# The other order of the experts and early lower results, with a fifth slot in the ring of split weight pairs, in the expert stage of a two-layer decoder trunk

## The reference

```
xn = rms_norm(x)                                   # 512 tokens, 1024 columns, float32
group  = the best of 4 groups (softmax p_group)
e1, e2 = the best two of the group's 4 experts, softmaxed and scaled by p_group
for e in 16 experts:
    hid = silu(xn @ w_gate[e]) * (xn @ w_up[e])    # 1024 -> 256
    y  += gates[:, e] * (hid @ w_down[e])          # 256 -> 1024
x = x + y
```

## Time and profile before

| | us |
|---|---|
| median of three runs (lowest, highest) | 1561.42 (1557.63, 1564.19) |
| the profiled execution's own time | 1558.49 |
| its span | 1556.6 |
| PE busy | 1458.1 |
| DVE busy | 935.9 |
| ACT busy | 866.0 |
| POOL busy | 457.7 |

### The profile page before, as it was taken

How to read it: one execution, slowest core, us unless ns; L and a number is a source line. 1 busy time by engine, 2 the same in 40 slices (tenths; PEclk the granted TensorE clock), 3 DMA queues, 4 the chain that set the end, 5 groups by cost and what they waited for, 6 DMA issues and landing times.

```text
span 1556.6 us, 22096 instructions
## 1 busy us (share of the span) xinstructions
PE 1458.1 (94%) x7676; PEld 1128.2 (72%) x7676; DVE 935.9 (60%) x1824; ACT 866.0 (56%) x1668; POOL 457.7 (29%) x638
## 2 busy tenths in 40 slices
PE   7999999999999996999699999999999999889993
PEld 6887777677777785777578877766777777667772
DVE  3555654644554446999754565645454535579996
ACT  4456655555453335888554655555554433558883
POOL 3414318410000024873104152284000000268210
PEclk9999999999999997999899999999999999989997
DMA  7822222142232366999675222211422332669995
GB/s 178 141 79 63 60 63 64 53 109 68 62 115 75 105 204 215 353 358 351 242 198 112 79 58 60 68 55 55 109 68 61 115 101 92 232 218 371 369 347 209
DMA packets 155381, 231.01 MB, mean 148 GB/s; under 512 B 20579, under 2 KB 89955, under 8 KB 155268
## 3 DMA queue, kind: packets, MB, share of 16 engines
q1 hardware_dynamic: 143780, 209.62, 44.8%
q0 software_dynamic: 10768, 17.80, 3.5%
q10 hardware_dynamic: 720, 2.16, 0.4%
HBM read 220.99 MB, written 29.69 MB: 161 GB/s over the span
## 4 chain that ended last, share of the span: by engine, by line
PE 71%; DVE 12%; ACT 5%; issue 4%; POOL 4%; DMA 4%; SPq 0%; ACTq 0%; DVEq 0%; POOLq 0%
PE bank L528 19%; PE bank L530 17%; PE bank L529 17%; PE bank L1526 4%; DVE xT L593 4%; PE bank L1511 3%; PE bank L1502 3%; PE bank L1504 2%; ACT xT L587 2%; DVE oT L937 1%; DVE gate_t L1937 1%; DMA ac<-xn_dram,tab_i 1%; PE bank L1558 1%; DMA q_c<-ytok 1%; DMA raw<-in_w_in_dram 1%
## 5 line engine op out<-in xcount | busy, mean ns | idle before, releaser
L528 PE MATMUL bank<-wh,xT 128*128 128x512 f32 (+1 forms) x960 | 398.7, 415 | 8.0 <-DVE gate_t L1937 4.6
L530 PE MATMUL bank<-wh,xT 128*128 128x512 f32 (+1 forms) x960 | 373.7, 389 | 0.0
L529 PE MATMUL bank<-wl,xT 128*128 128x512 f32 (+1 forms) x960 | 372.8, 388 | 0.0
L474 ACT ACTIVATE wh<-raw,gcol 128x512 fp32r<-128x512 f32 (+1 forms) x208 | 148.7, 716 | 203.8 <-PE bank L530 195.8
L481 DVE SCALAR_TENSOR_TENSOR wl<-raw,gcol,wh 128x512 fp32r<-128x512 f32 (+1 forms) x208 | 162.5, 783 | 136.3 <-ACT wh L474 128.9
L528 PEld LDWEIGHTS bank<-wh,xT 128*128 128x128 f32 x960 | 180.5, 188 | 75.1 <-issue 23.0
L530 PEld LDWEIGHTS bank<-wh,xT 128*128 128x128 f32 x960 | 180.1, 188 | 37.5
L529 PEld LDWEIGHTS bank<-wl,xT 128*128 128x128 f32 x960 | 181.1, 189 | 29.9 <-issue 1.4
L1875 DVE CUSTOM_DVE_ANT_0 prob<-bank,mask 128x128 f32<-128x128 f32 (+3 forms) x128 | 60.6, 489 | 192.3 <-PE bank L1502 103.0
L2197 POOL TENSOR_TENSOR rows<-x_rows,ac 128x512 f32<-128x512 f32 x16 | 21.9, 1404 | 509.9 <-DVE x_rows L1946 509.9
L1664 ACT ACTIVATE prob<-prob,nmax 128x128 f32<-128x128 f32 (+3 forms) x192 | 107.2, 560 | 113.2 <-DVE nmax L1875 112.9
(11 more groups left out here) (339 smaller groups left out, 2697.6 us busy)
## 6 DMA issues: line engine op xcount, KB each, us to landing
raw<-in_w_in_dram SPq DMA_DIRECT2D x192, 256.0 KB, 2.7
bqkv<-in_w_expert_gate_dram SPq DMA_DIRECT2D x64, 256.0 KB, 5.1
bqkv<-in_w_expert_up_dram SPq DMA_DIRECT2D x64, 256.0 KB, 6.5
bqkv<-in_w_expert_down_dram SPq DMA_DIRECT2D x32, 512.0 KB, 7.7
q_c<-in_w_expert_gate_dram SPq DMA_DIRECT2D x64, 256.0 KB, 5.8
q_c<-in_w_expert_up_dram SPq DMA_DIRECT2D x64, 256.0 KB, 7.7
head_odd<-in_w_expert_down_dram SPq DMA_DIRECT2D x32, 512.0 KB, 7.7
raw<-in_w_branch_dram SPq DMA_DIRECT2D x48, 256.0 KB, 2.6
```

Of the source, the lines that this page charges most:

```text
L474: nc.scalar.activation(wh[:, i % HL, 0:width], raw[:, i % RAW, 0:width], ACT.Copy, scale=piece_gain(i))\
L528: nc.tensor.matmul(out, lhs[0], rhs[0], start=start, stop=False)
L529: nc.tensor.matmul(out, lhs[0], rhs[1], start=False, stop=False)
L530: return nc.tensor.matmul(out, lhs[1], rhs[0], start=False, stop=stop)
```

## The change

1. **Order.** `ORDER` takes the experts as 0, 4, 8, 12, 1, 5, 9, 13, 2, ... 15, so that the four experts with the highest number of each group come last. Loads, gathers and scatters use `ORDER[e]`.
2. **Early lower results.** Block 0 of ytok is complete once twelve experts are scattered. SP reads its first tile in step 14 and the other three in step 15, ahead of the last scatters. DVE adds tile 0 in step 14, in the place of the rows that this step does not have, and tiles 1 to 3 after its steps. The two buffers of `back` are exchanged. Behind the last scatter four reads and four additions are left.
3. **Gate weights.** `gate_weights` is cut in two and done in steps 12 and 13, ahead of pair 3, and no longer behind the loop.
4. **A fifth slot.** The ring has five slots; the fifth lies in wh and wl, which the projections use outside the expert stage.
5. **Ahead of waits.** ACT and DVE take pair 4 ahead of the wait for the turned hidden rows, and pair 0 of the next step ahead of the silu.

```diff
+ORDER = [EG * (e % NG) + e // NG for e in range(NE)]
+LOW_DONE = NE - NG
...
         def pair_ring(e, j, par):
-            return j if is_const(e, -1) else (2 * par + j) % 4
+            return (0, 1, 4, 2, 3)[pair_no(e, j) % 5]
+
+        def pair_half(r, a):
+
+            return (wl if a else wh)[:, 0:2] if r == 4 else pair_w[:, r, a]
...
-            if j >= 4:
-                pair_multiplied(nc.scalar, e, j - 4)
-            elif is_const(e, 0):
-                pair_multiplied(nc.scalar, -1, j)
-            elif not is_const(e, -1):
-                pair_multiplied(nc.scalar, e - 1, j + 2)
+            if is_const(e, -1):
+                if j == 2:
+                    multiplied(nc.scalar, END[GID["out", 1]])
+            elif j == 5:
+                pair_multiplied(nc.scalar, e, 0)
+            elif not is_const(e, 0):
+                pair_multiplied(nc.scalar, e - 1, j + 1)
+            elif j:
+                pair_multiplied(nc.scalar, -1, j - 1)
...
+            def low_back(n):
+                sp.dma_start(back(n, 0), ytok_block(0, n)).then_inc(back_in[n], 16)
+
+            def step_and_low(e, par, half):
+                step(e, par, half)
+                if e == NE - 2:
+                    sp.wait_ge(xn_out, of(xn_out, 16 * NT))
+                    for q in range(2):
+                        sp.wait_ge(y_out[q], of(y_out[q], 16 * LOW_DONE // 2))
+                    low_back(0)
+                if e == NE - 1:
+                    for n in range(1, NT):
+                        low_back(n)
+
+            expert_steps(step_and_low)
             passed(pair_no(NE - 2, 3) + 1)
-            sp.wait_ge(y_out[0], of(y_out[0], 16 * NE // 2))
-            sp.wait_ge(y_out[1], of(y_out[1], 16 * (NE // 2 - 1)))
-            for n in range(EARLY):
-                sp.dma_start(back(n, 0), ytok_block(0, n)).then_inc(back_in[n], 16)
             overflow_sp(sp, layer)
             for par in range(2):
                 sp.wait_ge(y_out[par], of(y_out[par], 16 * NE // 2))
             for n in range(NT):
-                if n >= EARLY:
-                    sp.dma_start(back(n, 0), ytok_block(0, n)).then_inc(back_in[n], 16)
                 sp.dma_start(back(n, 1), ytok_block(1, n)).then_inc(last_in[n], 16)
...
         (ACT, step)
                 if not end:
                     pair_hi(e, 3, par, half)
+                    pair_hi(e, 4, par, half)
                 act.wait_ge(hid_turned, of(hid_turned, e + 1))
...
                 if not end:
-                    pair_hi(e, 4, par, half)
                     pair_hi(e, 5, par, half)
+                    pair_hi(e + 1, 0, 1 - par, half + par)
                     gate_silu(e + 1, 1 - par)
                     if not is_const(e, NE - 2):
                         rows_hi(e + 2, par)
-                    pair_hi(e + 1, 0, 1 - par, half + par)
...
         (DVE, step)
+                if e in (12, 13):
+                    gate_weights(dve, e - 12)
                 if not end:
                     pair_lo(e, 3, par, half)
+                    pair_lo(e, 4, par, half)
                 dve.wait_ge(hidT_hi, of(hidT_hi, e + 1))
...
                 if not end:
-                    pair_lo(e, 4, par, half)
                     pair_lo(e, 5, par, half)
+                    pair_lo(e + 1, 0, 1 - par, half + par)
                     silu(e + 1, 1 - par)
-                    if not is_const(e, NE - 2):
+                    if is_const(e, NE - 2):
+                        add_first(0)
+                    else:
                         rows_lo(e + 2, par)
-                    pair_lo(e + 1, 0, 1 - par, half + par)
                     pair_lo(e + 1, 1, 1 - par, half + par)
...
             expert_steps(step)
-            gate_weights(dve)
+            for n in range(1, NT):
+                add_first(n)
...
-            return rows[:, n, :] if k else q_c.rearrange("p h s -> p (h s)")[:, n * D:(n + 1) * D]
+            return q_c.rearrange("p h s -> p (h s)")[:, n * D:(n + 1) * D] if k else rows[:, n, :]
```

More of the change, by code:

```diff
@@ L37 @@
 LEAD = 2
-EARLY = 2
+ORDER = [EG * (e % NG) + e // NG for e in range(NE)]
+LOW_DONE = NE - NG
 NCH = 23
@@ L579, in pair_hi @@
             nc.scalar.wait_ge(landed, of(landed, count))
-            if j >= 4:
-                pair_multiplied(nc.scalar, e, j - 4)
-            elif is_const(e, 0):
-                pair_multiplied(nc.scalar, -1, j)
-            elif not is_const(e, -1):
-                pair_multiplied(nc.scalar, e - 1, j + 2)
-            nc.scalar.activation(pair_w[:, pair_ring(e, j, par), 0], pair, ACT.Copy).then_inc(pair_hi_ready, 1)
+            if is_const(e, -1):
[7 more added lines that the diff above has]
+                pair_multiplied(nc.scalar, -1, j - 1)
+            nc.scalar.activation(pair_half(pair_ring(e, j, par), 0), pair, ACT.Copy).then_inc(pair_hi_ready, 1)
         def pair_lo(e, j, par, half):
@@ L610, in gate_up @@
                 kt = 2 * j + k
-                mm = passes(out, (x_[:, 0, kt], x_[:, 1, kt]), (pair_w[:, r_, 0, k], pair_w[:, r_, 1, k]),
+                mm = passes(out, (x_[:, 0, kt], x_[:, 1, kt]), (pair_half(r_, 0)[:, k], pair_half(r_, 1)[:, k]),
                             kt == 0, kt == KD - 1)
@@ L616, in down @@
             for k in range(2):
-                mm = passes(out, (hidT[:, 0, k], hidT[:, 1, k]), (pair_w[:, r_, 0, k], pair_w[:, r_, 1, k]),
+                mm = passes(out, (hidT[:, 0, k], hidT[:, 1, k]), (pair_half(r_, 0)[:, k], pair_half(r_, 1)[:, k]),
                             k == 0, k == 1)
@@ L784, in step @@
                         passed(j + 1 if is_const(e, 1) else pair_no(e - 2, j) + 1)
-                        load_gate_up(sp, layer * NE + (e + 1), j, 1 - par, pair_in[1 - par][j])
+                        load_gate_up(sp, layer * NE + ORDER[e + 1], j, 1 - par, pair_in[1 - par][j])
                 if not is_const(e, 0) and not is_const(e, 1):
@@ L788, in step @@
                         passed(pair_no(e - 2, 4 + c) + 1)
-                        load_down(sp, layer * NE + e, c, par, pair_in[par][4 + c])
-            expert_steps(step)
+                        load_down(sp, layer * NE + ORDER[e], c, par, pair_in[par][4 + c])
+            def low_back(n):
[11 more added lines that the diff above has]
+            expert_steps(step_and_low)
             passed(pair_no(NE - 2, 3) + 1)
-            sp.wait_ge(y_out[0], of(y_out[0], 16 * NE // 2))
-            sp.wait_ge(y_out[1], of(y_out[1], 16 * (NE // 2 - 1)))
-            for n in range(EARLY):
-                sp.dma_start(back(n, 0), ytok_block(0, n)).then_inc(back_in[n], 16)
             overflow_sp(sp, layer)
@@ L1029, in home @@
                     pool.wait_ge(y_zero, of(y_zero, 16))
-                scatter(ysb[:, e % 2, :], home_i[:, e:e + 1], y_out[e % 2])
+                scatter(ysb[:, e % 2, :], home_i[:, ORDER[e]:ORDER[e] + 1], y_out[e % 2])
             for e in range(NE):
@@ L1034, in experts_pool @@
                     pool.wait_ge(xg_turned, of(xg_turned, 2 * (e - 1)))
-                gather(xg[:, e % 2, :], tab_i[:, e:e + 1], xg_in[e % 2])
+                gather(xg[:, e % 2, :], tab_i[:, ORDER[e]:ORDER[e] + 1], xg_in[e % 2])
                 if e >= 4:
@@ L1158, in overflow_slots, with gate_weights @@
                 chain(nc.vector.tensor_tensor(dst[:, NE:], marks[:, c, 0:n_ov], first_col, ALU.add))
-        def gate_weights(dve):
+        def gate_weights(dve, part):
             tt, ts = nc.vector.tensor_tensor, nc.vector.tensor_scalar
+            swap, keep = r1[:, 14, :], r1[:, 15, :]
+            if part:
+                chain(tt(r1[:, 25, :], r1[:, 23, :], r1[:, 5, :], ALU.mult))
+                chain(ts(keep, swap, -1.0, 1.0, ALU.mult, ALU.add))
+                for k in range(2):
+                    tt(r1[:, 28 + k, :], r1[:, 24 + k, :], keep, ALU.mult)
+                    chain(tt(r1[:, 30 + k, :], r1[:, 25 - k, :], swap, ALU.mult))
+                chain(tt(r1[:, 26:28, :], r1[:, 28:30, :], r1[:, 30:32, :], ALU.add))
+                return
             dve.wait_ge(r_act, of(r_act, 2))
@@ L1168, in gate_weights @@
             nc.vector.tensor_copy(r1[:, 24, :], r1[:, 23, :])
[L1169 to L1175, removed]
         def place_overflow(pool, part):
@@ L1345, in _ @@
                     for j in range(4):
-                        load_gate_up(sp, layer * NE + e, j, e, pair_in[e][j])
+                        load_gate_up(sp, layer * NE + ORDER[e], j, e, pair_in[e][j])
                     for c in range(2):
-                        load_down(sp, layer * NE + e, c, e, pair_in[e][4 + c])
+                        load_down(sp, layer * NE + ORDER[e], c, e, pair_in[e][4 + c])
                 for n in range(NT):
```

15 lines of the change are left out of this document (5 added, 10 removed).

## The result

| | before | after |
|---|---|---|
| median (lowest, highest), us | 1561.42 (1557.63, 1564.19) | 1552.03 (1551.90, 1553.05) |
| the profiled execution's own time, us | 1558.49 | 1552.03 |
| its span, us | 1556.6 | 1550.2 |

The forecast was 1554.6, and -6.8 between profiled executions.

What follows compares the result with a forecast made beforehand. PE, busy for 94% of the span, was taken as the bound, so time is won only where it waits. -1.9 + 2.3 - 3.5 - 3.7 = -6.8 us: 1551.7 against the profiled 1558.5, scaled 1554.6; range 1546 to 1561.

Steps and rivals of the forecast that it cites:

- Loop A: In a steady step ACT idles until hidden rows are turned, DVE trails, pair 0 reaches PE late; 0.51 us per step.
- loop B: Cycle of PE's down pair 4, ACT's first result half, pair 1, DVE, PE: 3.37 us of a 9.81 us step.
- Full pace (B): Rival: pair 1 is not late, steps reach PE's 9.38 us; -15 us, 1546 us; chance 0.17.
- PE's own 9.38 us: Steady step of layer 1: the length PE alone would need, without the 0.51 us lost at pair 0.
- The steps' term: Expert steps: 1.0 us in layer 1's 13 steps, 0.4 in its early steps, 0.5 in layer 0; sum -1.9.
- the claim for layer 0: Layer 0: PE already waits for the gather at 682.08, so only six steps behind it count, 0.5 us.
- Gate weights: Moved into steps 12 and 13, where DVE has no cover: cost 1.2 us per layer, 2.3 for two.
- The like case in the trace: Four overflow-slot operations delay pair 3 by 0.79 us, step 0.41 too long; room at pair 3 is 0.38 to 0.4.
- The ends: At each layer's end: shorter last scatter, fewer reads and additions behind it; -3.5 us in layer 0, -3.7 in layer 1.
- Transfers (C): Rival: transfers at 368 GB/s keep steps from shortening, the 1.9 us are lost; -4.9, 1556.5 us; chance 0.14.
- DVE's rows (D): Rival: DVE's rows, with 0.17 us of room, become late at pair 0; at 0.6 us +4, 1566; chance 0.06.
- the early reads (E): Rival: early reads land late or disturb the last weight loads, ends gain 0; 1562 us; chance 0.06.

Runs made afterwards that it cites:

- e: Changed kernel with ACT taking pair 1 of the next step ahead of the first result half; 1548.61 us, 0.9909 of the kernel before.
- f: Changed kernel with ACT taking pairs 1 and 2 of the next step ahead of both result halves; 1545.58 us, 0.9897 of the kernel before.
- h: Changed kernel with pairs 1 and 2 ahead of both result halves, gate weights ahead of the loop, overflow slots behind it; 1543.72 us, 0.9884.
- i: h with GpSimd's seven parts of slot work spread over steps 2 to 13 and the overflow table moved to step 14; 1543.40 us, 0.9885.
- c: Kernel before with only the fifth slot and the pairs ahead of waits; 1556.44 us, 0.9956.
- b: Changed kernel with the four-slot ring and old ACT and DVE order put back, keeping expert order, early reads and gate weights; 1559.27 us, 0.9978.
- the repeat: The changed kernel run again with no edit; 1552.74 us, 0.9931 of the kernel before.
- j: Changed kernel with layer 1's output writes issued only when all additions are done; 1554.65 us, 0.9962 of the kernel before.
- g: Changed kernel with pair 1 ahead of the first result half, gate weights ahead of the loop, overflow slots behind it; 1544.21 us, 0.9883.
- d: Changed kernel with both parts of the gate weights ahead of the loop; 1550.10 us, 0.9911 of the kernel before.
- l: b with all four additions of lower results behind the loop; 1555.25 us, 0.9952 of the kernel before.
- k: b with step 14's first addition put behind the low half of the last pair; 1559.21 us, 0.9985 of the kernel before.

## Why the prediction was right

- **Loop A goes, loop B takes over: shown.** The wait moved from pair 0 to pair 1 and from the hidden rows to the first result half, the step came out at 9.78 (forecast 9.81), in two pieces of 3.29 and 6.49 (forecast 3.37 and 6.46), and taking pair 1 out of the loop (e) gave 9.54. Full pace (B) was wrong for the change itself. PE's own 9.38 us was a little high: f, h and i have steps of 9.32.
- **The steps' term was too small.** Forecast -1.9. With the gate weights' 1.2 taken off, the loops of the changed kernel are 1.1 and 2.0 us shorter, together 3.1, and in c 4.3. Two pieces were left out: the step with the slots gains 0.15 (10.30 to 10.15 in layer 1) and the last 0.26 to 0.30, since pairs ahead of their waits help there too (c has both, b neither). And the claim for layer 0, that whatever the steps ahead of the late gather win, PE waits there, holds in one execution and not in the other: the step with the gather takes 10.20 before and 9.91 after, without a wait for the gather, but 10.51 in the repeat, with 0.5 of waiting. Steps 1 to 7 together win 0.6 us in the one and 0.3 in the other.
- **Gate weights: right.** Forecast 0.48 and 0.70 over a plain step, measured 0.47 and 0.72. The like case in the trace, the slots, gave the room at pair 3.
- **The ends were too large.** Forecast -3.5 and -3.7, measured -2.8 and -2.8 (-2.65 and -3.3 in the repeat). A last scatter alone takes 2.8 to 3.0 us here and not the 2.6 of the earlier trace rows: 0.3 us per layer. In layer 0 even the 0.63 us that it did win are given back: the read that the additions wait for takes 5.98 us in place of 5.34 and lands when it did before, at 778.42. What is left is the two additions' 2.6 and 0.2. Why the read takes longer stays open. In layer 1 the last read, beside the output's first writes, lands 7.97 us after its issue, at 1544.82, and the last addition starts behind it; 0.9 to 1.3 us of that are the writes' (j). They ran beside the reads before the change too, so this does not price the term's error.
- **The sum** came out at -6.4 against -6.8 since these two errors, 1.2 too little in the steps and 1.6 too much in the ends, nearly cancel. That part is luck. That the medians moved by 9.4 comes from the kernel before, whose profiled execution was 2.9 us under its median and the changed one's at it; the reason for that spread stays open, and the terms explain 6.4 us and not the 9.4.
- **Transfers (C)** did not bind: steps of 9.54 and 9.32 ran where 9.9 were to be the least. But i shows where the rival is right: over a whole layer, not in a step. The loads go at 345 to 375 GB/s in windows of 10 us whatever the step, and in i, which asks for 392, ACT waits for weights late in the loop. The Trainium skill, DMA: Bandwidth & Descriptors, section "Where 436 GB/s comes from", has some 358 GB/s for a core's HBM traffic; the page of the changed kernel shows 370 in three slices running, 3% above it, so the measurement decides, though the figure is near the pace at which i ran short.
- **DVE's rows (D) and the early reads (E):** no wait for pair 0 (but for 0.2 us in the first step of each layer) or for these reads is in the trace, and ACT waits for no weights in either layer, so the early reads of steps 14 and 15 delayed none. D and E were wrong.

The best versions tried are h and i, 1543.7 and 1543.4 us, 0.9884 and 0.9885 of the kernel before where the changed kernel is at 0.9931 to 0.9936, so 7 to 8 us under it: pairs 1 and 2 ahead of the result halves, gate weights and slots out of the loop. g, with pair 1 alone, is within 1 us of them, and in its profile 1.8 us are lost at layer 1's last product.

## What to carry to other kernels

When a loop of three engines is tuned by order, write down every cycle that closes through two in-order queues, with its length: cutting the longest gains only the distance to the next (0.10 us of 0.51 here), and the next was to be read from the same timeline. A change in two parts may hide a dependence: an operation of 1.28 us was harmless with one part and cost 1.9 us per layer without it, most of it by way of the clock. Before shortening steps further, divide the loop's bytes by the rate that its windows show, and count how long the buffers' lead can pay for the rest.

## What was not expected of the hardware

- TensorE's granted clock in the last down product: at 1.00 behind waits of 1.62 to 1.84 us (before, after, c, d, e, i, j, l), and at 1.2 GHz for most of the product behind 1.95 to 2.12 us (b and k, both layers) and 1.89 (g, layer 1), where passes come every 0.43 us and not every 0.23. It cost 1.8 to 2.1 us each time, the longer wait included. But at 1.00 too behind 2.08 (h, layer 1) and 2.23 (g, layer 0). How the chip decides is not settled by this.
- A gather that held TensorE for 4.0 us (h, layer 0; 3.9 in f) was followed by some 4 us at the lower clock, and the step grew by 6.5 us.
- The same code ahead of layer 0's experts took from 595.9 to 599.2 us in the profiled executions of these kernels, so a single profile can't show a gain of 1 or 2 us in the total; loops cut at their own first and last rows can.
- Four reads of 512 KB behind a scatter take 8.0 us to land when nothing else is in flight (j), and 8.9 to 9.3 beside the output's first writes.
